# A mixer's output projection as seven Strassen products, with weight sums made in DRAM

## Chip, cores and metric

The kernel runs on one core of a Trainium2 chip. The time is the device time of one execution in microseconds (us), taken as the median of several runs; lower is better. Five engines run their own instruction streams: TensorE (PE in the rows, PEld for its weight loads), VectorE (DVE), ScalarE (ACT), GpSimd (POOL) and SyncE (SP), which here only issues DMA transfers.

## The reference, cut to what matters

One decoder layer on a sequence of 512 tokens with a width of 2048, all in float32: attention and a state-space branch are gated and merged, then comes an output projection with a norm and a residual, then a SwiGLU feed-forward network (FFN).

```python
merged = sigmoid(gate_a) * attn_branch + sigmoid(gate_s) * ssm_branch     # (512, 2048)
x = x + rms_norm(merged @ w_out, norm_mix_post)                           # w_out (2048, 2048)
h = rms_norm(x, norm_ffn_pre)
f = (silu(h @ w_ffn_gate) * (h @ w_ffn_up)) @ w_ffn_down                  # w_ffn_down (5632, 2048)
return x + rms_norm(f, norm_ffn_post)
```

## The kernel before

**Products in three passes.** Each float32 operand is split into a high part (ScalarE copies it into a reduced format) and a low part (VectorE subtracts the high part from the original). A product is high x high + high x low + low x high, three matmuls of 128x512. Weights arrive by SP's DMA queue in a ring of four tiles of 512 KB (`raw`); `split_hi` on ScalarE and `split_lo` on VectorE make `w_hi` and `w_lo`, two deep. The semaphores `landed`, `hi_ready`, `lo_ready` and `piece_done` tie them together: a load waits until the piece four before it is split, a split until the piece two before it is multiplied.

**The stages around the change**, in the order in which every engine runs them:

- *The query, key and value stage.* After each load SP also issues a copy of 512 KB from `w_ffn_down` to `v_d`, DRAM to DRAM (`v_begin`).
- *The gated-unit (GLU) stage*, 32 pieces in 8 turns of four, 693 us to 867 us. Each piece has a load and a `v_begin`. At the end of each turn from the second on GpSimd stores `sig_g` to `gl_d` (line 2834). `gate_sums` on VectorE prepares the mixer's units.
- *The mixer's units*, 14 of them, 867 us to 1140 us: Strassen products of gate weights, 7 products each. SP loads 2 MB for a unit (`load_unit`, line 695) while the unit before is multiplied; VectorE forms block sums of them (lines 2172 to 2182). After each second unit VectorE merges two rows of tiles into `au_c` (`merge_ssm`), GpSimd stores them to `m_d` and reloads `au_c` and `gl_c`.
- *The output projection*, 1140 us to 1314 us. `merged` comes back whole from `m_d` into `mrg` and is split into `a_hi` and `a_lo` in six runs (`MRG_RUNS`). Then come 32 pieces of 24 matmuls, in four column blocks of 512 over all four chunks of 128 tokens (`piece_t`). Beside a block's successor ScalarE squares it for the norm and VectorE multiplies it by the gain. The last four pieces run chunk by chunk (`last_mix_pieces`), so that chunk c is complete while chunk c+1 is multiplied.
- *Weight sums for the down projection.* During the output projection GpSimd issues six turns of `v_turn`. A turn is up to four transfers that add 512 KB from DRAM onto a `v_d` block (`accum_op`); each turn waits for the landing of the one before. The other turns run beside the FFN's units, spread over a turn by waits on `product`.
- *The middle norm.* For each chunk: `mix_gain`, mean, root, `mix_residual` (which makes `x2`), a square of `x2`, root and `x2_scale`. Then TensorE transposes the scaled chunks by pairs (`pe_mid_turn`), ScalarE and VectorE make high and low parts of the result, and the first four FFN pieces are multiplied in halves (`pe_mid_piece`), chunks 0 and 1 first.
- *The FFN's units*, then the *down projection*, which is already seven Strassen products (Z1 to Z7) of 22 steps each: a step (`piece_d`) has 12 matmuls on a block of 256 K-rows, a load of 512 KB and one of 128 KB; VectorE combines finished products in SBUF beside later steps (`combine`).

TensorE, ScalarE, VectorE, GpSimd and SP each run a fixed order written out by hand, so an instruction that waits holds all behind it on its engine.

## Time and profile before

| | |
|---|---|
| median of 3 runs | 2623.95 us (2623.66 to 2624.27) |
| the profiled execution | 2623.74 us, its span 2622.0 us |
| TensorE busy | 2598.7 us (99%) |
| VectorE, ScalarE, GpSimd busy | 1735.6, 1055.9, 590.4 us |
| DMA | 504.20 MB, mean 192 GB/s |

Busy time is a share of the span. TensorE's clock is granted at full speed nearly throughout. Matmuls overlap, so the time of one is longer than the spacing between two. The DMA share is the mean busy share of the core's 16 DMA engines; packet time of a queue is given as a share of the same 16 engines.

### The profile page before, as it was taken

The page shows a single profiled execution, that of the slowest core. Times are in us where ns is not written, and L with a number is a line of the kernel's source. Part 1 is how long each engine was busy: PE and PEld are TensorE (multiplying, and loading weights), DVE is VectorE, ACT ScalarE, POOL GpSimd, SP SyncE. Part 2 cuts the span into 40 slices and gives each one's busy share as a digit, 9 for nine tenths or more (in the row PEclk, how much of TensorE's full clock was granted, in tenths as well). Part 3 has the DMA queues.
Part 4 walks back from the last instruction along what each step waited for, and adds up shares of the span by engine and source line. Part 5 has one row for each costly group of instructions (what it writes and reads, how often), then busy time and mean ns, then how long its engine had stood idle before and what let it go on. Part 6 is the DMA issues. An engine that isn't in the chain of part 4 may idle for free.

```text
span 2622.0 us, 38782 instructions
## 1 busy us (share of the span) xinstructions
PE 2598.7 (99%) x14213; PEld 2222.4 (85%) x14213; DVE 1735.6 (66%) x2121; ACT 1055.9 (40%) x1427; POOL 590.4 (23%) x828
## 2 busy tenths in 40 slices
PE   8999999999999999999999999999999999999998
PEld 7888888888888888888888888888888888888887
DVE  5233232243344899962477999999999997666677
ACT  5222231232422444442354444444444444555555
POOL 3979127771000000001101212212212211000000
PEclk9999999999999999999999999999999999999999
DMA  6477676527666444378734586676677655788777
GB/s 186 137 229 229 168 188 217 194 70 206 217 218 209 151 153 161 128 255 194 177 128 146 156 213 179 169 213 184 169 207 191 181 148 195 257 272 277 242 242 237
DMA packets 310580, 504.20 MB, mean 192 GB/s; under 512 B 29024, under 2 KB 238304, under 8 KB 308032
## 3 DMA queue, kind: packets, MB, share of 16 engines
q1 hardware_dynamic: 264456, 365.76, 42.7%
q0 software_dynamic: 28720, 118.48, 18.3%
q10 hardware_dynamic: 17288, 18.40, 2.3%
q8 instruction: 74, 1.21, 0.2%
q14 instruction: 42, 0.34, 0.0%
HBM read 448.60 MB, written 150.41 MB: 228 GB/s over the span
## 4 chain that ended last, share of the span: by engine, by line
PE 95%; DVE 3%; issue 1%; ACT 1%; ACTq 0%; DVEq 0%
PE ps L787 26%; PE ps L793 14%; PE ps L495 8%; PE ps L499 8%; PE ps L497 8%; PE ps L851 5%; PE ps L853 5%; PE ps L855 5%; PE ps L616 2%; PE ps L617 2%; PE ps L618 2%; PE ps L603 1%; PE ps L602 1%; PE ps L601 1%; PE ps L583 1%
## 5 line engine op out<-in xcount | busy, mean ns | idle before, releaser
L483 DVE TENSOR_TENSOR w_lo<-raw,w_hi 128x1024 fp32r<-128x1024 f32 x176 | 229.8, 1306 | 539.9 <-ACT w_hi L479 539.8
L479 ACT ACTIVATE w_hi<-raw 128x1024 fp32r<-128x1024 f32 x176 | 186.5, 1060 | 559.0 <-PE ps L499 346.5
L495 PE MATMUL ps<-a_both,w_hi 128*128 128x512 f32 x640 | 252.4, 394 | 0.1
L497 PE MATMUL ps<-a_both,w_hi 128*128 128x512 f32 x640 | 249.4, 390 | 0.0
L499 PE MATMUL ps<-a_both,w_lo 128*128 128x512 f32 x640 | 249.4, 390 | 0.0
L787 PE MATMUL ps<-a_both,w_hi 128*128 128x512 f32 x872 | 216.9, 391 | 0.0
L787 PEld LDWEIGHTS ps<-a_both,w_hi 128*128 128x128 f32 x872 | 160.3, 188 | 31.1
L787 PE MATMUL ps<-a_both,w_hi_b 128*128 128x512 f32 x640 | 159.2, 391 | 0.0
L717 ACT ACTIVATE w_hi<-raw 128x1024 fp32r<-128x1024 f32 x81 | 85.5, 1056 | 165.7 <-DVE raw L2182 76.3
L495 PEld LDWEIGHTS ps<-a_both,w_hi 128*128 128x128 f32 x640 | 120.2, 188 | 27.6 <-issue 1.8
L499 PEld LDWEIGHTS ps<-a_both,w_lo 128*128 128x128 f32 x640 | 120.2, 188 | 25.1
L497 PEld LDWEIGHTS ps<-a_both,w_hi 128*128 128x128 f32 x640 | 120.3, 188 | 23.9
L808 ACT ACTIVATE f_hi<-f_raw 128x256 fp32r<-128x256 f32 x151 | 63.1, 418 | 188.0 <-PE ps L855 187.9
L787 PEld LDWEIGHTS ps<-a_both,w_hi_b 128*128 128x128 f32 x640 | 117.7, 188 | 22.7
L2885 POOL TENSOR_TENSOR f_sums<-f_t 128x256 f32<-128x256 f32 x22 | 34.5, 1569 | 450.2 <-DVE f_t L2439 363.4
L787 PE MATMUL ps<-s_both,w_hi_b 128*128 128x512 f32 x480 | 119.4, 391 | 0.0
L787 PE MATMUL ps<-s_both,w_hi 128*128 128x512 f32 x480 | 119.4, 391 | 0.0
L851 PE MATMUL ps<-w_hi,f_hi 128*128 128x512 f32 x300 | 116.8, 389 | 1.5 <-DVE f_lo L812 1.5
L851 PE MATMUL ps<-w_hi_b,f_hi 128*128 128x512 f32 x304 | 118.3, 389 | 0.0
L853 PE MATMUL ps<-w_lo_b,f_hi 128*128 128x512 f32 x304 | 118.3, 389 | 0.0
L855 PE MATMUL ps<-w_hi_b,f_lo 128*128 128x512 f32 x304 | 118.3, 389 | 0.0
L853 PE MATMUL ps<-w_lo,f_hi 128*128 128x512 f32 x300 | 116.8, 389 | 0.0
(439 smaller groups left out, 6458.2 us busy)
## 6 DMA issues: line engine op xcount, KB each, us to landing
raw<-in_w_in SPq DMA_DIRECT2D x108, 512.0 KB, 4.5
v_d<-in_w_ffn_down SPq DMA_DIRECT2D x88, 512.0 KB, 5.2
raw<-in_w_ffn_gate SPq DMA_DIRECT2D x88, 512.0 KB, 10.8
raw<-v_d SPq DMA_DIRECT2D x88, 512.0 KB, 4.9
raw_b<-in_w_ffn_up SPq DMA_DIRECT2D x80, 512.0 KB, 5.4
raw<-in_w_ffn_down SPq DMA_DIRECT2D x66, 512.0 KB, 4.8
v_d<-in_w_ffn_down POOLq DMA_DIRECT2D x44, 512.0 KB, 8.8
v_d<-v_d POOLq DMA_DIRECT2D x44, 512.0 KB, 7.8
```

The costliest lines, as they stand in the source:

```text
L479: nc.scalar.activation(w_hi[:, m % 2, :], raw[:, m % 4, :], ACT.Copy).then_inc(hi_ready, 1)
L483: nc.vector.tensor_tensor(w_lo[:, m % 2, :], raw[:, m % 4, :], w_hi[:, m % 2, :].bitcast(F32), ALU.subtract).then_inc(lo_ready, 1)
L495: nc.tensor.matmul(o, wh[:, k, cols], x_hi[:, kt0 + k, :], start=first and k == 0, stop=False, skip_group_check=halves)
L497: nc.tensor.matmul(o, wh[:, k, cols], x_lo[:, kt0 + k, :], start=False, stop=False, skip_group_check=halves)
L499: mm = nc.tensor.matmul(o, wl[:, k, cols], x_hi[:, kt0 + k, :], start=False, stop=last and k == 3, skip_group_check=halves)
L717: nc.scalar.activation(by_kt(ph.hi[ph.slot(j, i)]), operand(ph, j, i), ACT.Copy).then_inc(unit_hi, 1)
L787: mm = nc.tensor.matmul(wide, wh[:, k, :], ph.x_both[p][k], start=starts, stop=False, skip_group_check=True)
L793: mm = nc.tensor.matmul(o, wl[:, k, :], ph.x_hi[p][:, k, :], start=opens and p < 4 and k == 0, stop=False, skip_group_check=True)
L808: nc.scalar.activation(dst, f_raw[:, n % 4, :], ACT.Copy).then_inc(f_hi_ready, 1)
L851: nc.tensor.matmul(o, f_hi[n % 2][:, toks], wh[:, d, :], start=opens, stop=False, skip_group_check=True)
L853: nc.tensor.matmul(o, f_hi[n % 2][:, toks], wl[:, d, :], start=False, stop=False, skip_group_check=True)
L855: mm = nc.tensor.matmul(o, f_lo[n % 2][:, toks], wh[:, d, :], start=False, stop=closes, skip_group_check=True)
```

## The change

The output projection is computed as seven Strassen products over halves of tokens, K-rows and columns. K is cut into 8 pairs of 128-row tiles (`WO_PAIRS`), so there are 7 x 8 = 56 steps of 12 matmuls, in the order O1, O6, O7, O5, O4, O3, O2. Four of the products need weight sums and four need sums of `merged`.

- Weight sums: SP begins them by copies of `w_out` to `vo_d` (the first 32 of `v_begin`), which moves 32 later copies for `v_d` to the mixer's units, six after each unit's loads. GpSimd adds onto `vo_d` in ten turns (`vo_turn`): seven in the GLU stage behind the stores to `gl_d`, three in the mixer's units between the reloads of `au_c` and `gl_c`, where four turns of `v_turn` follow. Two more `v_turn` come at the start of the FFN; none is left in the output projection.
- Sums of `merged`: GpSimd makes four per pair (`merged_sums`) and stores them to `ms_d`.
- The stage: each step loads 128 KB of `ms_d` or `m_d` and 512 KB of weights; ScalarE and VectorE split both. `mrg` is not reloaded. Products are combined in `o_t` by 32 operations on VectorE and ScalarE; the last three steps are kept and multiplied chunk by chunk.
- The middle norm: chunks 2 and 3 come first, chunks 0 and 1 second. The scaling by the inverse root moves from VectorE to ScalarE (`act_x2_scale`), gains and residuals are done in halves of 1024 columns.

The core of the diff:

```diff
+WO_PAIRS = KT // 2
+WO_STEPS = 7 * WO_PAIRS
+B_FF = B_WO + WO_STEPS
 def v_begin(sp, i):
+            v, j, l = ((0, 0, 0), (2, 0, 1), (1, 1, 1), (3, 1, 0))[i % 4]
+            if i < 4 * WO_PAIRS:
+                sp.dma_start(vo_d[v][i // 4], w_block(w_out, j, l, i // 4)).then_inc(vo_begun, 16)
+            else:
+                m = i // 4 - WO_PAIRS
+                sp.dma_start(v_d[v][m], w_block(w_fd, j, l, m)).then_inc(v_begun, 16)
...
+            for u in range(MIX_UNITS):
+                g, j = u // 4, u % 4
+                load_unit(sp, MIX, g, j, w_in, 512 * g + (GA_COL, GS_COL)[j % 2] + 256 * (j // 2 + 1))
+                for i in range(88 + 6 * u, min(88 + 6 * u + 6, 4 * (WO_PAIRS + PAIRS))):
+                    v_begin(sp, i)
...
+            for n in range(WO_STEPS):
+                load_out(sp, n)
...
+            def vo_turn(t):
+                if t:
+                    pool.wait_ge(v_added, 16 * v_adds(t, WO_PAIRS))
+                else:
+                    pool.wait_ge(vo_begun, 16 * 4 * WO_PAIRS)
+                if t < WO_PAIRS:
+                    v_add(vo_d[0], t, w_block(w_out, 0, 1, t))
+                    v_add(vo_d[2], t, w_block(w_out, 1, 1, t))
+                if 1 <= t <= WO_PAIRS:
+                    v_add(vo_d[1], t - 1, vo_d[0][t - 1])
+                if 2 <= t < WO_PAIRS + 2:
+                    v_add(vo_d[3], t - 2, vo_d[1][t - 2])
...
             for it in range(1, 8):
                 pool.wait_ge(gl_made, it + 1)
                 pool.dma_start(gl_d[:, 2 * it:2 * it + 2, :].rearrange("p a n -> p (a n)"), sig_g[:, :]
                                ).then_inc(gl_stored, 16)
+                vo_turn(it - 1)
...
                     pool.dma_start(m_d[:, 2 * it - 2:2 * it, :], au_c[:, :, :]).then_inc(m_stored, 16)
+                    store_merged_sums(it - 1)
                     pool.wait_ge(m_stored, 16 * it)
...
                 pool.dma_start(au_c[:, :, :], au_d[:, kts, :]).then_inc(au_in, 16)
+                if it <= 3:
+                    vo_turn(6 + it)
+                else:
+                    v_turn(it - 4)
                 pool.wait_ge(gl_stored, 16 * it)
                 pool.dma_start(gl_c[:, :, :], gl_d[:, kts, :]).then_inc(gl_in, 16)
...
+            for n in range(WO_STEPS - ENDS):
+                piece_o(pe, n)
+            out_end_pieces(pe)
...
+            out_end_hi(act, 0)
+            act_x2_square(act, 0)
+            out_end_hi(act, 1)
+            out_end_hi(act, 2)
+            act_mid_root(act, 2, 0)
+            act_x2_scale(act, 0)
+            for i in range(4):
+                act_mix_square(act, 8 + i, i // 2, 2 + i % 2, AFTER_O3)
+            act_x2_square(act, 1)
             for m in (B_FF, B_FF + 1):
                 kept_split_hi(act, m)
+            act_mid_root(act, 3, 1)
+            act_x2_scale(act, 1)
+            split_hi(act, B_FF + 2, 0)
+            split_hi(act, B_FF + 3, 0)
+            act_mix_square(act, 12, 0, 0, AFTER_O3 + 1)
+            act_mix_square(act, 13, 0, 1, AFTER_O3 + 2)
+            act_mid_root(act, 4, 2)
...
+            out_end_lo(dve, 0)
+            mix_root(1, 1)
+            mix_residual(1, 0, 4)
+            out_end_lo(dve, 1)
+            x2_mean(0)
+            out_end_lo(dve, 2)
+            mix_residual(1, 1, 4)
+            x2_invert(2, 0)
+            mix_gain(0, 1, 10)
+            mix_gain(1, 1, 12)
+            last_product(0, 0)
+            last_product(0, 1)
+            x2_mean(1)
             for m in (B_FF, B_FF + 1):
                 kept_split_lo(dve, m)
+            x2_invert(3, 1)
+            split_lo(dve, B_FF + 2, 0)
+            split_lo(dve, B_FF + 3, 0)
+            mix_gain(0, 0, 14)
+            mix_mean(2)
+            last_product(1, 0)
+            last_product(1, 1)
```

## Rows read from the trace of the kernel before

**Rows 1.** The page, chain that ended last: share of the span by engine.
```profile
PE 95%; DVE 3%; issue 1%; ACT 1%; ACTq 0%; DVEq 0%
```

**Rows 2.** Output projection's first matmul line; ns min/median/max, first and last start.
```profile
L616 PE MATMUL ps<-w_hi,a_both x224: 388/389/467, 1140.3 to 1292.0; 128*128 128x512 f32 x112
```

**Rows 3.** Windows: busy us of PE, PEld, DVE, ACT, POOL; clock, DMA share, GB/s.
```profile
742.00:850.00 108.00, 108.00 (x478) 89.49 (x477) 52.16 (x45) 33.35 (x33) 2.36 (x5) 1.00 0.65 213
850.00:871.00 21.00, 21.00 (x102) 17.69 (x101) 13.23 (x13) 6.71 (x7) 0.53 (x1) 1.00 0.39 127
871.00:910.00 39.00, 39.00 (x227) 34.48 (x226) 36.18 (x44) 18.43 (x25) 1.60 (x3) 1.00 0.55 188
910.00:1105.00 195.00, 195.00 (x1123) 172.38 (x1122) 187.99 (x225) 89.82 (x121) 8.02 (x15) 1.00 0.44 148
1314.00:1348.00 34.00, 31.55 (x255) 29.79 (x254) 23.75 (x48) 20.09 (x45) 0.58 (x1) 1.00 0.41 156
2290.00:2400.00 110.00, 110.00 (x487) 91.12 (x486) 73.46 (x93) 54.91 (x80) 1.62 (x3) 1.00 0.81 271
```

**Rows 4.** The adds' DMA queue, 1206 to 1250 (packets, MB, share); one load.
```profile
q0 software_dynamic: 1152, 4.19, 53.1%
...
L451 SPq DMA_DIRECT2D raw<-in_w_out x1: 373/373/373, 1208.4 to 1208.4; - x1
...
DMA to landing us min/median/max: 12.0/12.0/12.0
```

**Rows 5.** SP's DMA queue in the GLU stage, 785 to 829.
```profile
q1 hardware_dynamic: 5481, 8.50, 59.1%
```

**Rows 6.** SP's DMA queue in the mixer's units, 910 to 1105.
```profile
q1 hardware_dynamic: 21120, 20.97, 32.9%
```

**Rows 7.** Timeline of issues: start us, us, queue; SP's, then GpSimd's.
```profile
837.24 0.38 SPq L451 DMA_DIRECT2D raw<-in_w_glu_g  x1
...
853.69 5.81 SPq L695 DMA_DIRECT2D raw<-in_w_in  x2
...
867.69 2.85 SPq L695 DMA_DIRECT2D mix_raw_b<-in_w_in  x4
...
881.47 2.04 SPq L695 DMA_DIRECT2D raw<-in_w_in  x4
...
872.36 0.53 POOL L2834 DMA_DIRECT2D gl_d<-sig_g  x1 [21.39 <-DVE sig_g L2102]
```

**Rows 8.** Timeline: readers of loads, then TensorE around the stage's end.
```profile
856.65 1.06 ACT L479 ACTIVATE w_hi<-raw 128x1024 fp32r<-128x1024 f32 x1 [4.38 <-PE ps L499]
...
864.27 1.22 DVE L2175 TENSOR_TENSOR raw<-raw 128x1024 f32<-128x1024 f32 x1
...
884.83 1.22 DVE L2175 TENSOR_TENSOR mix_raw_b<-mix_raw_b 128x1024 f32<-128x1024 f32 x1
...
904.33 1.22 DVE L2175 TENSOR_TENSOR raw<-raw 128x1024 f32<-128x1024 f32 x1
...
1314.48 0.27 PE L1001 MATMUL ps<-ident,o_t 128*128 128x128 f32 x1
...
1318.24 0.39 PE L515 MATMUL ps<-a_both,r_hi 128*128 128x256 f32 x1 [0.34 <-DVE a_both L1868]
```

**Rows 9.** Timeline of the middle norm, ScalarE and VectorE.
```profile
1298.35 0.60 ACT L1365 ACTIVATE sq_t<-ps 128x512 f32<-128x512 f32 x1 [2.42 <-PE ps L568]
...
1305.60 1.90 ACT L1371 ACTIVATE o_t<-x 128x2048 f32<-128x2048 f32 x1
...
1299.07 0.69 DVE L2326 TENSOR_TENSOR o_t<-ps,gain_b 128x512 f32<-128x512 f32 x1 [1.51 <-ACT sq_t L1365]
...
1305.93 2.35 DVE L2336 SCALAR_TENSOR_TENSOR x<-o_t,stat,x 128x2048 f32<-128x2048 f32 x1
...
1316.52 1.66 DVE L1868 SCALAR_TENSOR_TENSOR a_both<-ps,gain_t,a_both 128x256 fp32r<-128x256 f32 x4
```

**Rows 10.** The page's group of the FFN's pair sums on GpSimd.
```profile
L2885 POOL TENSOR_TENSOR f_sums<-f_t 128x256 f32<-128x256 f32 x22 | 34.5, 1569 | 450.2 <-DVE f_t L2439 363.4
```

More of the change, by code:

```diff
@@ L398, in build @@
         gl_in = sem("gl_in")
-        mrg_in = [sem(f"mrg_in{h}") for h in range(2)]
+        vo_begun = sem("vo_begun")
+        x2_inverse = sem("x2_inverse")
         gs_made = sem("gs_made")
@@ L857, in piece_d @@
[L857 to L870 removed]
+            step(pe, n, B_DN, WO_STEPS, f_hi, f_lo, q, m == 0 and q != Z2, m == PAIRS - 1)
@@ L878, in end_pieces @@
                 for i in range(ENDS):
-                    part(1, d, i)
+                    mm = end_part(1, d, i, e_hi, e_lo, ef_hi, ef_lo)
+                mm.then_inc(down, 1)
         def w_tiles(w, row_tiles, rows0, cols0, n):
@@ new lines, in _, with mix_gain, mix_mean @@
+            out_lo(dve, 2)
+            out_lo(dve, 3)
+            def mix_gain(c, half, squares):
+                dve.wait_ge(mix_sq, squares)
+                dve.wait_ge(gb_in[0], 16)
+                cols = slice(1024 * half, 1024 * half + 1024)
+                tt(o_t[:, c, cols], o_t[:, c, cols], gain_b[:, cols], ALU.mult).then_inc(mix_gained, 1)
+            def mix_mean(i):
+                c = OUT_ORDER[i]
+                dve.wait_ge(mix_sq, (4, 8, 14, 16)[i])
+                link(nc.vector.tensor_reduce(stat[:, 0, c:c + 1], sq_part[:, :, c], AX, ALU.add))
+                ts(stat[:, 1, c:c + 1], stat[:, 0, c:c + 1], 1.0 / D, EPS, ALU.mult, ALU.add).then_inc(rstd_in, 1)
@@ new lines, in mix_root, with mix_residual @@
+            def mix_root(n, i):
+                c = OUT_ORDER[i]
+                dve.wait_ge(rstd_sqrt, CLS + n + 1)
+                link(nc.vector.reciprocal(stat[:, 2, c:c + 1], stat[:, 1, c:c + 1]))
+            def mix_residual(i, half, gains):
+                c, cols = OUT_ORDER[i], slice(1024 * half, 1024 * half + 1024)
+                dve.wait_ge(mix_gained, gains)
+                dve.wait_ge(x_again, 16 * CLS)
+                added = stt(x2[:, c, cols], o_t[:, c, cols], stat[:, 2, c:c + 1], x2[:, c, cols], ALU.mult, ALU.add)
+                if half:
+                    added.then_inc(x2_ready, 1)
@@ new lines, in x2_mean, with x2_invert, last_product @@
+            def x2_mean(i):
+                c = OUT_ORDER[i]
+                dve.wait_ge(sq_done, CLS + i + 1)
+                ts(stat[:, 1, c:c + 1], stat[:, 0, c:c + 1], 1.0 / D, EPS, ALU.mult, ALU.add).then_inc(rstd_in, 1)
+            def x2_invert(n, i):
+                c = OUT_ORDER[i]
+                dve.wait_ge(rstd_sqrt, CLS + n + 1)
+                nc.vector.reciprocal(stat[:, 2, c:c + 1], stat[:, 1, c:c + 1]).then_inc(x2_inverse, 1)
+            def last_product(c, d):
+                if c == 0 and d == 0:
+                    dve.wait_ge(mixed, 1)
+                else:
+                    dve.wait_ge(piece_done, B_FF - ENDS + 2 * c + d)
+                combine(AFTER_O3 + 2 * c + d, o_part(c, d), o_part(c, d), down_bank(O2, c, d), ALU.add)
@@ new lines, in _ @@
+            for n in range(4, WO_STEPS - ENDS):
+                out_lo(dve, n)
+                dve_beside_out(n)
+            out_end_lo(dve, 0)
[11 more added lines that the diff above has]
+            x2_mean(1)
@@ L2553, in finish_part @@
                     ALU.add).then_inc(out_ready, 1)
-            def combine(done, out, a, b, op):
-                dve.wait_ge(combined, done)
-                tt(out, a, b, op).then_inc(combined, 1)
             def dve_beside(n):
@@ L2828, in _, with store_merged_sums @@
+            def store_merged_sums(m):
+                pool.wait_ge(gl_stored, 16 * 7)
+                pool.wait_ge(ms_stored, 16 + 32 * (m - 1))
+                merged_sums(m, au_c, *(ms_three[:, i, :] for i in range(3)), ms_last[:, :])
+                pool.dma_start(ms_d[m, :, 0:3, :], ms_three[:, :, :]).then_inc(ms_stored, 16)
+                pool.dma_start(ms_d[m, :, 3, :], ms_last[:, :]).then_inc(ms_stored, 16)
             pool.wait_ge(au_copied, 8)
```

590 lines of the change are left out of this document (309 added, 281 removed).

## The prediction

> **What bounds the kernel now.** The page comes first. TensorE is busy for 99% of the span and makes 95% of the chain that ended last [rows 1]; so the end moves only with TensorE's work or with a wait that reaches it. The profiled execution took 2623.74 us for a span of 2622.0, 1.7 us outside it, and lies 0.2 us under the median of 2623.95; I add to and subtract from that median. A difference of 0.2% (5.2 us) is about what this kernel's measurement can tell from none.
>
> The second view gives the stage that is replaced. Its 768 matmuls of 128x512 run from 1140.2 to the first transpose of the middle norm at 1314.5 with TensorE busy throughout [rows 2, 8]: 174.2/768 = 0.2268 us each. Nothing but TensorE limits that stage.
>
> The third view is the DMA share of each stage, since the change multiplies DRAM traffic. It is 0.65 in the gated-unit (GLU) stage from 742 to 850, 0.39 to 871, then 0.55 and 0.44 in the mixer's units, while TensorE has no gap in any of them [rows 3]. The last rows show how the middle norm hides: its ScalarE and VectorE steps run per chunk under matmuls, so that the stretch from 1314 to 1348 has only 2.45 us of idle TensorE [rows 3].
>
> **The change, part by part.**
>
> *Matmuls.* 56 steps of 12 matmuls are 672 in place of 768: 96 x 0.2268 = **-21.8 us**. This is certain if nothing waits.
>
> *Loads of the new stage.* A step needs 640 KB in 12 x 0.2268 = 2.72 us. The down projection already has this very shape, and ran with no TensorE gap at a share of 0.81 with a spill beside it [rows 3]. I cost these loads at nothing; without that cover each late load would show as a gap before its step.
>
> *Start of the stage.* VectorE has the last merge (two 1.2 us operations after a sigmoid, the width of the row of 884.8 [rows 8]) before the split of step 2; by its queue that split ends some 1 us after step 2 could start. I take **+1**, bounds 0 and, if both of the last splits come one operation later, 3.
>
> *DRAM adds.* What one costs is read in the stage where six turns of them stand today. The two turns between 1206 and 1250 have 8 adds, whose queue took 53.1% of 44 us: 2.9 us of all 16 engines each, 11.7 us for a turn of four [rows 4]. In the GLU stage SP's queue spends 59.1% of 44 us on 8 pairs of load and copy, 3.25 us a pair [rows 5]; in the mixer's units its 40 loads take 32.9% of 195 us, 1.6 each [rows 6]. So a DRAM copy costs 1.65.
>
> The change puts turns of 2, 3, 4, 4, 4 and 4 adds behind the stores of the GLU stage, some 21.8 us apart; the seventh and last store is issued at 872.4 [rows 7], so the first at about 742, and behind the seventh turn stands an eighth at once; and SP issues six copies (9.9 us) after the loads of each of the first five units. Of each 21.8 us a full turn wants: 0.65 x 21.8 = 14.2 used today, + 11.7 = 25.9. That is more than there is. Backlog: about 1 after the turn of 763.5, 5 at 807, 9 at 829, 13 at 850.4. The last GLU load is issued at 837.2 and first read at 856.7 [rows 7, 8], so with 4 us to land and 3 before TensorE misses it the slack is some 18 us, and these pieces just pass. Then:
> - unit 0's last load is issued at 859 [rows 7] and VectorE reads it from 864.3 [rows 8]; product 1 starts late once it lands after 867. Behind 13 of backlog, one turn (11.7), a store (1.3) and 3.2 of loads, from 850.4 on, it lands near 880: **13 us late**.
> - unit 1's loads (issued 867.7 [rows 7], the second half first read at 884.8 [rows 8]) stand behind six copies: 9.9 + 6.4, and the turn of 872.4 with its neighbours, 14. From 880 that is 910, against 884.8 + 13: **12 more**.
> - unit 2's loads (issued 881.5 [rows 7]) stand behind six copies, with the eighth turn: 910 + 16.3 + 12.8 = 939; the second half is read at 904.3 [rows 8], now + 25 = 929: **10 more**.
> - unit 3's, 19.5 us on, are due near 958 and land near 957; unit 4's, with two adds, are late by some **2**. After that the backlog melts: the share of 0.44 leaves 22 us free in 39 [rows 3].
>
> The sum is 37. It has every load land last of what was issued before it. One load issued 2.3 us after a burst of four adds took 12.0 us to land [rows 4], and the burst with the loads in it some 4 x 2.9 + 3 x 1.5 = 16, so a load is nearly last but not quite. I take **+32**; bounds: 0 (the slack absorbs all; below nothing is excluded, since TensorE has no idle there to give back) and 45 (GLU pieces late too). The Trainium skill (DMA: Bandwidth & Descriptors, section on queues, rings and completion order) says that each DMA engine takes turns between its queue rows, a whole packet at a time. By that rule the adds would lengthen a load by the packets interleaved and not by the whole burst, and my 37 would be some 26; the landing of 12.0 us is nearer to the burst.
>
> *Sums of the merged rows on GpSimd.* Four operations at the 1.57 us of the FFN's pair sums [rows 10] and two stores before the next reload of au_c: 7 us more, where the reader of that reload comes some 19 us after the merge before it. They run beside VectorE, which is busy 187.99 of 195 us there [rows 3]. Cost 0, upper bound 5 (the 7 us of VectorE's idle time gone, less a little).
>
> *The adds that leave the output stage.* TensorE had no gap there [rows 3], so this returns 0. Two turns now fall at the FFN's first pair sums; the share there leaves room: 0, up to 3.
>
> *The tail and the middle norm.* This is the part to follow in the queues. Durations [rows 9]: ScalarE 2.0 for a square of a chunk with its sum read, as a scale of one about 1.9, 0.75 for a square of a quarter; VectorE 2.35/2 = 1.2 for a residual of half a chunk, 0.7 for a combine, 1.66/4 = 0.4 for the residue of a turned tile; and 1.06 on ScalarE for a weight half [rows 8]. Times from E, where matmul 672 would end unhindered. VectorE has beside steps 50 to 52 a combine, two half-chunk residuals and a gain over 2.72 us a step, 1.7 us of slack: the splits for the last three steps are done near -7.3, -4.3 and -2.5, where TensorE wants them at -8.2, -6.8 and -5.4. The last matmul ends at **+3**.
>
> Chunk 3 (second in the new order) is scaled only after: residual of chunk 3 (-1.3), scale of chunk 2 (+0.9), four quarter squares (+3.9), square of chunk 3 (+5.9), two weight splits (+8.0), VectorE's residues for them and the reciprocal (+9.4), scale (+11.4). The first transposes wait for it: idle from +3 to +11.5. Then ScalarE has two weight splits and two squares (+14.9), VectorE gain, mean and the last two combines (+17.7), which free the banks of transposes 4 and 5; the turned tiles are ready and piece 0 starts at **+19.5**. Today it starts at 1318.2, 3.8 after the end of the matmuls [rows 8]. Between, chunks 0 and 1 still need residual, square, scale: waits of 2.4, 2.6 and 0.8 us at pieces 1, 3 and the second transposes, less some 1.3 that today's pieces wait. In all (19.5 - 3.8) + 4.5 = **+20**, the tail's 3 within it; bounds 8 (if the scale of chunk 3 is ready at once, and only the last two chunks' chain remains) and 26.
>
> Sum: 2624 - 21.8 + 1 + 32 + 20 = **2655 us**.
>
> **Rivals.**
> - *DMA absorbs it.* What speaks for it: loads have a unit of lead, and a share is no hard limit. Against: every share above is time of all 16 engines, and 0.65 + 0.54 is over one. Then 2624 - 21.8 + 1 + 20 = **2623**, no change; chance 0.14.
> - *The norm hides and only DMA costs*: the tail and norm cost 5; 2624 - 21.8 + 1 + 32 + 5 = **2640**; chance 0.12.
> - *Faster.* The saving of matmuls stands because neither reaches TensorE: the loads land before their readers, and chunks 2 and 3 are normed before the last steps end. It decides on whether chunk 3's scale comes before +5 and unit 1's loads before 885. 2624 - 21.8 + 1 + 5 = **2608**; chance 0.17. For it: chunks 2 and 3 are complete 22 us before the end; against it: the four squares and two splits placed ahead of that scale.
> - *My case*, both: **2655**, own range 2632 to 2680; chance 0.57.
>
> **The numbers.** The range goes from 2612 (leaving out most of the faster case) to 2680 (the upper bounds of either large cost). Faster by over 0.2% is the faster case and a quarter of the first rival: 0.21; within 0.2%: 0.07, about half of the first rival; slower: 0.72.
>
> **What would show it.** Matmuls of the output stage: 672 at 0.227, some 153 us. TensorE's gaps between 850 and 990: 32 us if the adds and copies count, with ScalarE or VectorE named as waiting for a load; none if they are absorbed. The DMA share from 785 to 950 should be near 0.95. Between the last output matmul and piece 0: some 16 us; transposes waiting for ScalarE's scale of o_t. The prediction is wrong if the share from 785 to 910 stays under 0.9, or if the first middle transpose follows the last matmul at once.

## The result, and the profile after

The changed kernel takes 2666.59 us (median of 4 runs, 2664.46 to 2667.43) against 2623.8 us before it: 1.016 times as long, 95% interval 1.0148 to 1.0173. The forecast was 2655 us with a range of 2612 to 2680 and a chance of 0.72 for slower. The sign and the range held; how the sum came about did not hold everywhere. The profiled execution has a span of 2664.5 us, 42.5 more than before's 2622.0.

The first view answers to [rows 3]: the stages in windows (same columns).

```profile
742.00:850.00 108.00, 108.00 (x478) 89.41 (x478) 52.15 (x46) 33.35 (x33) 16.94 (x22) 1.00 1.00 283
850.00:871.00 21.00, 18.16 (x80) 14.79 (x79) 8.09 (x8) 3.18 (x3) 3.96 (x5) 0.99 1.06 305
871.00:910.00 39.00, 31.91 (x160) 27.41 (x159) 27.03 (x32) 15.52 (x19) 8.51 (x11) 0.83 1.04 297
910.00:949.00 39.00, 31.16 (x162) 26.96 (x161) 28.08 (x32) 12.81 (x16) 6.48 (x8) 0.87 1.01 337
949.00:1105.00 156.00, 151.07 (x858) 132.52 (x857) 151.49 (x174) 68.32 (x92) 30.52 (x38) 0.99 0.68 210
1179.00:1341.00 162.00, 155.47 (x671) 126.51 (x672) 118.19 (x156) 90.17 (x144) 8.49 (x12) 0.99 0.79 264
1341.00:1391.00 50.00, 35.05 (x260) 31.93 (x259) 32.17 (x62) 32.92 (x63) 0.54 (x1) 0.86 0.34 127
```

The DMA share is 1.00 from 742 to 850 in the GLU stage, where it was 0.65, and above 1.0 from there to 949. From 850 to 949 TensorE is idle for 17.8 us (2.84 + 7.09 + 7.84), where it had no gap, and its granted clock is down to 0.83 and 0.87 of full speed from 871 on. Who is waited for is in the next view, the timeline of TensorE (what ended the idle time stands in brackets), and in VectorE's waits from 860 to 950 (us in total, times, longest):

```profile
870.17 3.24 PE L830 MATMUL ps<-a_both,w_hi 128*128 128x512 f32 x8 [2.84 <-ACT w_hi L760]
...
896.03 3.75 PE L830 MATMUL ps<-a_both,mix_hi_b 128*128 128x512 f32 x8 [6.83 <-DVE sg L2336]
...
926.07 2.04 PE L836 MATMUL ps<-a_both,w_lo 128*128 128x256 f32 x8 [7.84 <-DVE sg L2336]
```

```profile
DVE mix_t_sum L2259 <- issue: 18.8, 2, 9.9
DVE mix_t_sum L2259 <- DMA raw<-in_w_in: 8.8, 1, 8.8
```

There are three gaps, one for each of the first units, as the prediction had them, and the load of a unit's weights is what VectorE lacks. The profile names the load at one of its three waits only; at the other two it names nothing ("issue"). But these operations start at 892.9 and 923.0, and the second load of the unit, issued at 869.3 and 896.3, took 23.6 and 26.6 us to land, which is 892.9 and 922.9 (before, these loads took 3.5 to 7.6 us). Behind each gap the matmuls run at half clock for a while. That shows in the rows too: eight matmuls of 128x512 take 3.24 and 3.75 us, where the same row at full clock reads 2.0.

The pace of the units is read from the stores of the merged pairs: count, first and last start. Before, then after:

```profile
L2840 POOL DMA_DIRECT2D m_d<-au_c x6: 536/536/538, 915.6 to 1110.8; - x6
```

```profile
L3027 POOL DMA_DIRECT2D m_d<-au_c x6: 543/564/564, 940.1 to 1149.0; - x6
```

The first store is 24.6 us late: 17.8 of idle time and some 7 of slower matmuls. That is the DMA term. But from the first store to the sixth it is 208.9 us in place of 195.2, so that another 13.7 us come in after the backlog is gone (share 0.68). The prediction has nothing there. The timeline of VectorE and of GpSimd at one of these stores says what it is:

```profile
1063.26 2.71 DVE L765 TENSOR_TENSOR w_lo<-raw,w_hi 128x1024 fp32r<-128x1024 f32 x1
1065.89 1.76 DVE L2269 TENSOR_TENSOR raw<-raw 128x1024 f32<-128x1024 f32 x1
1067.57 1.76 DVE L2259 TENSOR_TENSOR mix_t_sum<-mix_raw_b 128x1024 f32<-128x1024 f32 x1
1069.25 1.21 DVE L765 TENSOR_TENSOR mix_lo_b<-raw,mix_hi_b 128x1024 fp32r<-128x1024 f32 x1
...
1063.43 0.76 POOL L2996 TENSOR_TENSOR ms_three<-au_c 128x256 f32<-128x256 f32 x1
1064.12 0.75 POOL L2997 TENSOR_TENSOR ms_three<-au_c 128x256 f32<-128x256 f32 x1
1064.95 1.61 POOL L2999 TENSOR_TENSOR ms_three<-au_c,ms_three 128x256 f32<-128x256 f32 x1
1066.64 1.61 POOL L3001 TENSOR_TENSOR ms_last<-ms_three,au_c 128x256 f32<-128x256 f32 x1
```

VectorE's operation of this shape takes 1.22 us, here 2.71, 1.76 and 1.76 while GpSimd subtracts: 2.6 us lost for each set of four subtractions.

The new output stage runs from 1179.0 to the first transpose at 1341.35: 162.3 us against 174.2. The 672 matmuls alone are 152.4, so 9.9 are waits: 6.5 us idle in the window above, 1.4 in seven matmuls at half clock (0.43 us apart in place of 0.23) behind the longest of these gaps, and 2.0 in wider spacing here and there. In the middle the timelines of TensorE and ScalarE read:

```profile
1341.12 0.39 PE L927 MATMUL ps<-we_hi,wef_lo 128*128 128x512 f32 x1
...
1349.41 1.76 PE L1077 MATMUL ps<-ident,o_t 128*128 128x128 f32 x7 [7.79 <-ACT o_t L1450]
...
1354.86 2.33 PE L1077 MATMUL ps<-ident,o_t 128*128 128x128 f32 x8 [3.70 <-DVE o_t L2360]
1357.22 0.58 PE L524 MATMUL ps<-a_both,w_hi_b 128*128 128x256 f32 x1
```

```profile
1336.94 2.01 ACT L1450 ACTIVATE o_t<-x,stat 128x2048 f32<-128x2048 f32 x1 [2.54 <-DVE stat L2419]
...
1341.92 1.89 ACT L1437 ACTIVATE o_t<-x 128x2048 f32<-128x2048 f32 x1
...
1347.35 2.00 ACT L1450 ACTIVATE o_t<-x,stat 128x2048 f32<-128x2048 f32 x1 [1.46 <-DVE stat L2419]
```

Between the two scales (L1450) lie the four quarter squares, chunk 3's square and two weight splits, in that order; the transposes wait for the second scale. Piece 0 starts 16.1 us after the last output matmul. From the first transpose to the first matmul behind the middle pieces it is 49.6 us (1341.4 to 1391.0) against 34.1 (1314.5 to 1348.5). The transposes by themselves, first and last start, are a shorter measure of the same stretch, 28.2 us before and 43.7 after:

```profile
L1001 PE MATMUL ps<-ident,o_t x64: 270/273/328, 1314.5 to 1342.7; 128*128 128x128 f32 x64
```

```profile
L1077 PE MATMUL ps<-ident,o_t x64: 270/273/477, 1341.4 to 1385.1; 128*128 128x128 f32 x64
```

So the 42.5 us are: DMA 24.6, units after that 14.1 (to the output stage's start), output stage -11.9 (-21.8 + 9.9), middle +15.6, rest 0.1.

### The profile page after: what moved, and what is told of

It reads as the page before. It is cut to its first block, busy times and chain, and to the rows that moved or that the text cites. A ratio compares the mean times of both kernels' runs of the same rounds, so it can differ in the third digit from the quotient of the medians.

```text
span 2664.5 us, 39011 instructions
## 1 busy us (share of the span) xinstructions
PE 2594.7 (97%) x14117; PEld 2212.0 (83%) x14117; DVE 1803.4 (68%) x2224; ACT 1100.8 (41%) x1509; POOL 665.8 (25%) x909
## 4 chain that ended last, share of the span: by engine, by line
PE 47%; DVE 2%; ACT 1%; issue 0%; DVEq 0%; ACTq 0%
PE ps L830 19%; PE ps L836 10%; PE ps L891 5%; PE ps L893 5%; PE ps L895 5%; PE ps L504 1%; PE ps L508 1%; PE ps L506 1%; ACT o_t L1437 0%; DVE x_b L2683 0%; PE ps L524 0%; PE ps L528 0%; PE ps L526 0%; ACT o_t L1450 0%; PE ps L1077 0%
## 5 line engine op out<-in xcount | busy, mean ns | idle before, releaser
L492 DVE TENSOR_TENSOR w_lo<-raw,w_hi 128x1024 fp32r<-128x1024 f32 x146 | 192.6, 1320 | 449.7 <-ACT w_hi L488 449.6
L488 ACT ACTIVATE w_hi<-raw 128x1024 fp32r<-128x1024 f32 x146 | 154.5, 1059 | 451.4 <-PE ps L508 346.2
L760 ACT ACTIVATE w_hi<-raw 128x1024 fp32r<-128x1024 f32 x81 | 85.6, 1056 | 174.3 <-DVE raw L2269 81.8
L508 PEld LDWEIGHTS ps<-a_both,w_lo 128*128 128x128 f32 x640 | 120.1, 188 | 25.4
L836 PEld LDWEIGHTS ps<-a_both,w_lo 128*128 128x128 f32 x872 | 114.2, 193 | 12.5 <-DVE w_lo L765 8.0
L836 PE MATMUL ps<-a_both,w_lo 128*128 128x256 f32 x872 | 116.8, 285 | 7.8 <-DVE sg L2336 7.8
```

What stands on the lines that cost most here:

```text
L488: nc.scalar.activation(w_hi[:, m % 2, :], raw[:, m % 4, :], ACT.Copy).then_inc(hi_ready, 1)
L492: nc.vector.tensor_tensor(w_lo[:, m % 2, :], raw[:, m % 4, :], w_hi[:, m % 2, :].bitcast(F32), ALU.subtract).then_inc(lo_ready, 1)
L508: mm = nc.tensor.matmul(o, wl[:, k, cols], x_hi[:, kt0 + k, :], start=False, stop=last and k == 3, skip_group_check=halves)
L760: nc.scalar.activation(by_kt(ph.hi[ph.slot(j, i)]), operand(ph, j, i), ACT.Copy).then_inc(unit_hi, 1)
L836: mm = nc.tensor.matmul(o, wl[:, k, :], ph.x_hi[p][:, k, :], start=opens and p < 4 and k == 0, stop=False, skip_group_check=True)
```

## The experiments

Measured beside these runs, before took 2623.8 to 2624.1 us. "First store" and "last store" are those of the two rows above; 915.6 and 1110.8 before, 940.1 and 1149.0 after.

### Is it the DRAM traffic? Traffic alone, and a part of it moved

**e1_traffic**: the kernel before, with the copies and adds where the change puts them.

```diff
             for it in range(1, 8):
                 pool.dma_start(gl_d[...], sig_g[:, :]).then_inc(gl_stored, 16)
+                vo_turn(it - 1)
...
+                for i in range(88 + 6 * u, min(88 + 6 * u + 6, 4 * (WO_PAIRS + PAIRS))):
+                    v_begin(sp, i)
```

> The kernel before, with the change's DRAM traffic and nothing else of it: the copies of the output weights ahead of those of the down weights (so six copies stand behind the loads of each of the first units), the turns of adds behind the GLU stage's stores and beside the mixer's units, no turns in the output stage. The sums of the output weights are made and not used; the output projection and the norm are those of before. Theory (the 16 DMA engines are asked for more than they have from 785 on): the first gated unit's end comes 24 to 28 us late with DMA shares of about 1.0 from 763 to 950, and the time is 2648 to 2654. First rival (the lateness up to 940 us comes from the added work on the engines, not from the transfers): within 3 us of 2624. Second rival (transfers are late, but the turns that left the output stage give something back there): below 2645.

Measured: 2658.37 us, ratio 1.0136 (1.0119 to 1.0153). Its windows from 742 on:

```profile
742.00:850.00 108.00, 108.00 (x479) 89.41 (x478) 51.97 (x45) 33.47 (x33) 17.10 (x22) 1.00 1.00 282
...
871.00:910.00 39.00, 26.73 (x130) 22.90 (x131) 24.13 (x28) 12.77 (x16) 8.47 (x11) 0.78 1.03 291
...
949.00:1105.00 156.00, 156.00 (x899) 137.86 (x898) 150.22 (x181) 72.16 (x96) 17.97 (x26) 1.00 0.68 208
```

The first store is at 941.0, 25.4 late, with the same shares and the same fall of the clock; the transfers alone do it. After 949 there is no gap: the later drift is not theirs. The time is 4 us over what was expected, because this kernel, which still reloads the merged rows before its output stage, waits 5.4 us for VectorE's split there, at 1172, with a turn of four adds and the reload issued from 1142 to 1156. That the adds are its cause is only argued.

**e3_copies_later**: the changed kernel with the 32 copies behind the mixer's unit loads moved to the middle stage's loads.

```diff
-                for i in range(88 + 6 * u, min(88 + 6 * u + 6, ...)):
-                    v_begin(sp, i)
             for k in range(16):
                 load(sp, B_FF + k, ...)
+                for i in (88 + 2 * k, 89 + 2 * k):
+                    v_begin(sp, i)
```

> The changed kernel, with the 32 copies that stand behind the unit loads of the mixer moved to the loads of the middle stage (two behind each), where the DMA share is 0.36 to 0.43. Theory of the prediction (the copies make units 1 and 2 late, 22 of 37 us by its count, and the adds unit 0): the first pair of units comes 12 to 18 us earlier than in the changed kernel, and the time is 2646 to 2654. Rival (the adds alone take what there is, and the copies only ride along): not below 2661.

Measured: 2660.55 us, the median of three runs (2653.75, 2660.55, 2663.97), ratio 1.0126 (1.0106 to 1.0147); a fourth run of 12720.78 us, for which the record has no cause, is left out. The first store came at 925.7, 14.4 earlier, as the theory said, and the lead was still 12.0 us at the last middle transpose. In the profiled run, the slowest of the three, only 2.3 us of it are left at the end. Windows from 1400 on:

```profile
1400.00:1440.00 40.00, 40.00 (x178) 33.14 (x177) 21.31 (x14) 11.21 (x10) 10.92 (x9) 1.00 1.01 305
1460.00:1480.00 20.00, 12.98 (x64) 10.87 (x63) 10.13 (x13) 5.63 (x8) 0.00 (x0) 0.83 0.97 261
```

Copies and turns 4 and 5 of the adds now meet there at a share of 1.01, a load of the FFN lands 7.0 us late for TensorE, and the clock falls: the same mechanism at another place. The copies are worth 14.4 of the 24.6 us and the adds 10.2, but copies moved as a block take most of their cost along. The time decides nothing: it lies between the theory's range and the rival's, with one run inside the theory's. The landmarks show that the cause was right and that the gain was mostly lost again.

### The drift after 949: GpSimd's arithmetic

**e2_sums**: the kernel before, with `merged_sums` and its stores: one set at 722.8 in the GLU stage, six beside the pairs of units. **e6_stores_only**: the same stores without the subtractions. **e10_sums_twice**: the subtractions of e2_sums made twice.

```diff
                     pool.dma_start(m_d[:, 2 * it - 2:2 * it, :], au_c[:, :, :]).then_inc(m_stored, 16)
+                    store_merged_sums(it - 1)
```

In e6_stores_only `store_merged_sums` is this, where `t` is `au_c` seen as four rows of 256:

```diff
-                merged_sums(m, au_c, *(ms_three[:, i, :] for i in range(3)), ms_last[:, :])
-                pool.dma_start(ms_d[m, :, 0:3, :], ms_three[:, :, :]).then_inc(ms_stored, 16)
+                pool.dma_start(ms_d[m, :, 0:3, :], t[:, 0:3, :]).then_inc(ms_stored, 16)
```

and in e10_sums_twice the four subtractions stand in a loop:

```diff
+                for r in range(2):
                     tt(s1, f21, f22, ALU.subtract).then_inc(ms_made, 1)
                     tt(s3, f11, f21, ALU.subtract).then_inc(ms_made, 1)
```

> The kernel before, with GpSimd's four subtractions of the merged rows and their two stores to DRAM beside each pair of units (seven sets), and nothing else of the change; the sums are not used. Theory (VectorE's operations take longer while GpSimd's run, and VectorE has only 7 us of idle time in 195): VectorE operations next to a set show 1.7 to 2.7 us in place of 1.22, each pair of units grows by 1 to 2 us once the idle time is gone, and the time is 2629 to 2635. Rival (what grew by 13.5 us between 940 and 1149 in the changed kernel came from late transfers): within 1.5 us of 2624.

> The kernel before with the same stores to DRAM as in e2_sums and without GpSimd's subtractions (the stores read the merged rows themselves; nothing reads what they write). It tells the arithmetic from the transfers and from the later reload of au_c. Theory (GpSimd's arithmetic slows VectorE's): within 2 us of 2623.9. Rival (the stores, or the reload that comes later behind them, made e2_sums slower): 2630 or more.

> e2_sums with each set of four subtractions made twice (same operands, same results, not used), the stores once. Theory (each set takes some 2.5 us from VectorE, whose idle time in the units is 1.4 us a pair; the cost goes with the number of subtractions beyond it): e2_sums gave 10.9 us over before, twice the sets give 26 to 32 us over it, 2650 to 2656. Rival (the cost is one of order, the reload of au_c being late behind the sums, so that it grows by GpSimd's own 6 us a pair only where that reaches a reader): below 2643.

| | us | last store | ratio (95%) |
|---|---|---|---|
| e6_stores_only | 2623.75 | 1110.5 | 0.9999 (0.9990 to 1.0009) |
| e2_sums | 2634.79 | 1119.1 | 1.0041 (1.0027 to 1.0055) |
| e10_sums_twice | 2643.37 | 1126.0 | 1.0073 (1.0056 to 1.0090) |

The transfers cost nothing and the arithmetic 10.9 us. Windows of 40 us, first of e2_sums, then of e6_stores_only:

```profile
990.00:1030.00 40.00, 38.24 (x218) 33.38 (x218) 39.03 (x45) 16.82 (x23) 7.38 (x9) 1.00 0.47 152
```

```profile
990.00:1030.00 40.00, 40.00 (x231) 35.27 (x230) 38.61 (x48) 18.65 (x25) 2.70 (x5) 1.00 0.47 157
```

VectorE is busy longer and does less (45 operations in place of 48). Neither e2_sums nor e10_sums_twice has a wait of VectorE for the reload of `au_c` among its rows from 910 to 1140, so a late reload isn't the cause there.

For twice the sets I had expected 26 to 32 us. It gave 19.6, at the edge of what the rival allowed. The rows say why. In e2_sums the six sets beside the units stretch VectorE's operations by 2.5 us each (the fifth by 1.6), 14.2 in all, of which 10.9 reached the end. The repeats in e10_sums_twice add only 1.1 us each, 21.2 in all, of which 19.6 reached the end. So VectorE's idle time absorbs 3 us at most, and a repeat is cheaper than a first set, because part of it falls beside operations that aren't stretched. In e10_sums_twice, VectorE and then GpSimd:

```profile
1091.45 0.41 DVE L2260 TENSOR_TENSOR mix_q<-mix_p,ps 128x256 f32<-128x256 f32 x1
1091.90 0.42 DVE L2262 TENSOR_TENSOR mix_q<-mix_q,ps 128x256 f32<-128x256 f32 x1
1092.35 1.25 DVE L2266 TENSOR_TENSOR sg<-sg,mix_q 128x512 f32<-128x512 f32 x1
...
1091.61 0.74 POOL L2841 TENSOR_TENSOR ms_three<-au_c 128x256 f32<-128x256 f32 x1
1092.31 0.74 POOL L2842 TENSOR_TENSOR ms_three<-au_c 128x256 f32<-128x256 f32 x1
```

The two operations with an input from PSUM (`ps`) keep their 0.41 us beside a running subtraction. The next one, which reads two SBUF tiles, takes 1.25 us in place of 0.69.

### The middle norm

**e4_norm_order**: the changed kernel, order of the two engines' steps alone.

```diff
-            for i in range(4):
-                act_mix_square(act, 8 + i, i // 2, 2 + i % 2, AFTER_O3)
             act_x2_square(act, 1)
-            for m in (B_FF, B_FF + 1):
-                kept_split_hi(act, m)
+            act_mix_square(act, 8, 0, 2, AFTER_O3)
             act_mid_root(act, 3, 1)
+            act_mix_square(act, 9, 0, 3, AFTER_O3)
             act_x2_scale(act, 1)
+            ...
+            act_mid_turn(act, 0, range(4))
+            for m in (B_FF, B_FF + 1):
+                kept_split_hi(act, m)
```

> The changed kernel, with the middle norm's steps in another order on ScalarE and VectorE: chunk 3's square and scale ahead of the quarter squares and of the weight splits, the last combines ahead of the gains, chunk 0 before chunk 1, the first turned tiles ahead of the splits. Theory (the first transposes wait for work queued ahead of chunk 3's scale, piece 0 for what is queued ahead of the turned tiles): the idle before the first transposes falls from 7.8 to about 3.5, piece 0 starts 9 to 10 us after the last output matmul in place of 16, and the time is 2658 to 2662. Rival (the chain from the last combine through the banks sets piece 0, whatever the order; or chunks 0 and 1 are then late by what is won): within 2 us of 2666.6.

Measured: 2665.85 us (2661.51 to 2667.73), not told from 2666.6, as the rival had it in its second form (chunks 0 and 1 are then late by what is won). TensorE's timeline:

```profile
1344.13 2.15 PE L1077 MATMUL ps<-ident,o_t 128*128 128x128 f32 x11 [2.78 <-ACT o_t L1450]
...
1349.86 0.55 PE L524 MATMUL ps<-a_both,w_hi_b 128*128 128x256 f32 x1 [1.28 <-DVE w_lo_b L548]
...
1363.21 1.12 PE L1077 MATMUL ps<-ident,o_t 128*128 128x128 f32 x4 [3.83 <-DVE a_both L1955]
```

Piece 0 starts 7.4 us earlier, so the order of the queue was its cause. Then a turned tile that stands behind chunk 0's square on ScalarE is late by 3.8 us, and the pieces run at half clock twice in place of once. Most of the gain is given back in the same stage.

### The same transfers, spread

**e5_spread**: the changed kernel, the same copies and adds at another pace: the adds for `w_out` in smaller bursts, the 32 copies and all adds for the down weights moved out of the mixer's units to the FFN.

```diff
-                vo_turn(it - 1)
+                vo_adds(*((0, 2), (2, 4), (4, 6), (6, 7), (7, 8), (8, 9), (9, 10))[it - 1])
...
-                if it <= 3:
-                    vo_turn(6 + it)
-                else:
-                    v_turn(it - 4)
+                vo_adds(*((10, 14), (14, 18), (18, 22), (22, 26), (26, 29), (29, 31), (31, 32))[it - 1])
...
+                    if g <= 8:
+                        v_begin(sp, 88 + 4 * (g - 1) + j)
...
+                v_turn(m + 1, PROD0 + 14 * m + 85 if 2 <= m < PAIRS - 2 else None)
```

**e7_spread_norm**: e5_spread with the norm's order of e4_norm_order, tiles 8 to 11 turned earlier.

```diff
             act_mix_square(act, 15, 1, 1, AFTER_O2)
+            act_mid_turn(act, 0, range(8, 12))
             act_x2_square(act, 2)
-            act_mid_turn(act, 0, range(8, 12))
```

**e8_no_sums**: e7_spread_norm with the stores of e6_stores_only; it leaves out the sums of the merged rows, so the output isn't the reference's. **e9_adds_first**: e7_spread_norm, with the adds issued ahead of the sums and the turns of the FFN one pair earlier.

```diff
                     pool.dma_start(m_d[:, 2 * it - 2:2 * it, :], au_c[:, :, :]).then_inc(m_stored, 16)
+                    vo_adds(*adds)
                     store_merged_sums(it - 1)
...
-                v_turn(m + 1, PROD0 + 14 * m + 85 if 2 <= m < PAIRS - 2 else None)
+                v_turn(m + 2, PROD0 + 14 * m + 85 if 2 <= m < PAIRS - 2 else None)
```

> The changed kernel with the same DRAM copies and adds, spread out: behind the stores of the GLU stage two, two, two and then one add each, beside the mixer's units four, four, four, four, three, two and one in place of four each and six copies behind each unit's loads; the 32 late copies stand four to a group behind the loads of the FFN's units, and the adds for the down weights run one turn for each of the FFN's pairs. Theory (the DMA engines were asked for more than they have in one stretch; the amount as such can be hidden): DMA share under 0.95 in every window from 742 to 1150, no TensorE gap over 2 us and no half clock from 850 to 990, first store of a merged pair at 915 to 920, time 2636 to 2644. Rival (what is moved comes back as late loads where it now stands, as it did with the 32 copies moved as one block): above 2652.

> e5_spread with the middle norm's steps reordered once more: as in e4_norm_order, and tiles 8 to 11 turned on ScalarE before chunk 0's square, the later weight split of VectorE behind them. Theory (in e4_norm_order 5 of the 7.5 us won at piece 0 were given back in one wait of 3.8 us for turned tile 9 and its half clock): no gap over 1 us between piece 0 and the first transposes of chunks 0 and 1, time 3 to 6 us under e5_spread. Rival (ScalarE and VectorE are full there, so that any order gives the same end): within 1.5 us of e5_spread.

> e7_spread_norm without GpSimd's sums of the merged rows: the stores take the merged rows as they are, so that the four products that want the sums compute something else. All transfers and matmuls stay. Theory (the sums cost VectorE's time in the units, 10.9 us in the kernel before): 8 to 12 us under e7_spread_norm, the stores of merged pairs 39.0 us apart again in place of 41 to 44. Rival (with the transfers spread, VectorE's idle time hides them): within 2 us of e7_spread_norm.

> e7_spread_norm with two changes of order on GpSimd's queue: beside the mixer's units the adds are issued right behind the store of the merged pair and ahead of the sums and the reload, and in the middle and the FFN the turns for the down weights run one pair earlier, so that none of four adds is left for the start of the down projection. Theory (in e5_spread and e7_spread_norm the sums put the adds 6 us later, where they met the next unit's load: VectorE waited 3.2 us for it in each of three pairs; and the last turns made a load of the down projection late by 2.6 us): pairs 40.5 to 42 us apart in place of 43.8, the output stage starts at 1148 to 1153 in place of 1160.6, the rest 3 to 4 us shorter, time 2632 to 2639. Rival (the sums cost 20 us once the transfers are spread, wherever the adds stand): above 2643.

| | us | first, last store | output stage from | ratio (95%) |
|---|---|---|---|---|
| e5_spread | 2651.19 | 915.4, 1129.8 | 1160.5 | 1.0101 (1.0084 to 1.0118) |
| e7_spread_norm | 2647.63 | 915.8, 1129.9 | 1160.6 | 1.0096 (1.0079 to 1.0113) |
| e8_no_sums | 2627.19 | 915.6, 1110.8 | 1140.1 | 1.0011 (1.0001 to 1.0020) |
| e9_adds_first | 2637.60 | 915.4, 1124.2 | 1154.0 | 1.0052 (1.0035 to 1.0068) |

With the transfers spread the first store is where it was before the change: all 24.6 us of the DMA term are gone from there. They aren't all gone from the time: behind the last middle transpose e5_spread takes 1283.6 us, where before takes 1279.3, with a wait of TensorE of 2.5 us at 2239.8, in the down projection, that before doesn't have. Windows of e5_spread:

```profile
742.00:850.00 108.00, 108.00 (x478) 89.42 (x477) 52.13 (x46) 33.34 (x33) 9.37 (x13) 1.00 0.84 252
...
871.00:910.00 39.00, 39.00 (x226) 34.46 (x225) 36.16 (x44) 18.46 (x25) 5.93 (x8) 1.00 0.92 255
```

The time is 7 us over what was expected all the same, since each of the first three pairs of units now took 44 us where GpSimd's sums account for 2 over 39. e8_no_sums shows that the sums set off all of it: without them every store is within 0.05 us of before's, and the kernel is 20.4 us faster. That is twice what the sums cost alone, because they also put the four adds 6 us later, where they met the next unit's load. In e5_spread's waits of VectorE from 970 to 1000:

```profile
DVE mix_t_sum L2259 <- DMA raw<-in_w_in: 3.2, 1, 3.2
```

e8_no_sums also says what the rest of the change is worth when neither DMA nor sums cost anything in the units. Its output stage takes 158.1 us (16.1 saved), its middle 42.0 us from first to last transpose (13.8 lost), and 4.5 are lost behind that: the norm alone eats most of the saving.

e9_adds_first takes part of that back: a pair in 41.8 us, the output stage 6.6 earlier, 10.0 us in all, and behind the last middle transpose it takes 1279.4 us, as before. The adds ahead of the reload have a price of their own: VectorE now waits for `au_c`, 7.3 us in three times. e7_spread_norm gained 3.6 us in the median, with ranges that overlap (2644.1 to 2652.3, and 2648.0 to 2652.6), and not where I expected it: from the first to the last transpose it took 42.8 us, e5_spread 43.7, as chunk 1's scale was late by 5.0 us instead. What the two profiles differ by lies in the output stage ahead, 156.8 us in place of 160.7, which the edit doesn't touch. There e5_spread has a gap of 2.05 us at 1205.0, behind a load of `vo_d` for which ScalarE waited 4.2 us (1.9 in e7_spread_norm, without a gap), and seven matmuls at half clock behind it. Why that load landed earlier in one of two executions is open.

### A version that pays

**e11_dma_sums**: e9_adds_first, where the sums of pairs 1 to 6 are made without GpSimd's arithmetic, and where four quarter squares fill ScalarE's waits before the last output matmul.

```diff
+                        nc.scalar.activation(ms_three[:, 0:2, :], au_c[:, :, quad[1]], ACT.Copy, scale=-1.0)...
+                        nc.scalar.activation(ms_three[:, 2, :], au_c[:, 1, quad[0]], ACT.Copy, scale=-1.0)...
+                        nc.scalar.activation(ms_last[:, :], au_c[:, 1, quad[1]], ACT.Copy)...
...
+                    ms_add(m, slice(1, 4), ms_three[:, 0, :], 3)
+                    ms_add(m, slice(0, 1), ms_three[:, 1, :], 1)
...
             out_end_hi(act, 2)
+            act_mix_square(act, 8, 0, 2, AFTER_O3)
+            act_mix_square(act, 9, 0, 3, AFTER_O3)
+            act_mix_square(act, 10, 1, 2, AFTER_O3)
             act_mid_root(act, 2, 0)
```

**e12_two_bursts**: e11_dma_sums, with two of each four adds behind the pair's last sum.

```diff
-                    vo_adds(*adds)
+                    vo_adds(adds[0], min(adds[0] + 2, adds[1]))
...
                     ms_add(m, slice(3, 4), ms_three[:, 2, :], 1)
+                    if adds[1] > adds[0] + 2:
+                        vo_adds(adds[0] + 2, adds[1])
```

> e9_adds_first with two changes. First, the sums of the merged rows of pairs 1 to 6 are no longer made by GpSimd: ScalarE, which is busy 18 of 39 us there, writes negated copies of three quarter rows (and one plain copy), and the sums arise in DRAM by accumulating transfers, seven quarter rows a pair; GpSimd still makes the first and the last set. Second, in the middle norm the four quarter squares whose inputs are complete early go into ScalarE's waits before the last matmul, and VectorE scales chunk 1 into its residual earlier. Theory (VectorE loses its time to GpSimd's arithmetic, not to the transfers): pairs 39.0 to 39.6 us apart in place of 40 to 43, output stage from 1141 to 1144; the middle (first to last transpose) 36 to 40 us in place of 42.8; time 2616 to 2624, so the change as a whole would just begin to pay. Rival (the added transfers, some 5 us of all engines a pair, or the later reload of au_c make loads late again): above 2628.

> e11_dma_sums with the adds for the output weights split: two behind the store of a merged pair, the other two behind the last of the pair's sums, some 30 us later. In e11_dma_sums VectorE's operations kept their 1.22 us, but it waited 3.9 to 4.3 us for the reload of au_c, which was issued behind four adds, and TensorE for it. Theory (the reload lands in time behind two adds): no such wait over 1 us, pairs 39.0 to 40.2 us apart, the output stage starts at 1141 to 1146 in place of 1152.4, time 2619 to 2624. Rival (the accumulating transfers of the sums themselves keep the reload late): within 3 us of 2630.

e11_dma_sums measured 2630.10 us, ratio 1.0024 (1.0015 to 1.0033), as the rival had it. The operations of VectorE keep 1.22 us, and the middle takes 36.2 us; but in its waits from 880 to 1145 the first row, which e9_adds_first had with 7.3 us, has grown:

```profile
DVE au_c L2309 <- DMA au_c<-au_d: 11.6, 4, 4.3
```

The reload of the pair stood behind four adds. e12_two_bursts measured 2619.46 us (2614.89 to 2623.94), ratio 0.998 (0.997 to 0.9989): 4.6 us less than before it. Its windows and its transposes:

```profile
871.00:910.00 39.00, 39.00 (x226) 34.47 (x225) 36.18 (x45) 18.46 (x25) 5.96 (x8) 1.00 0.90 249
...
949.00:1105.00 156.00, 156.00 (x898) 137.83 (x897) 150.01 (x181) 76.05 (x108) 40.41 (x49) 1.00 0.92 236
```

```profile
L1077 PE MATMUL ps<-ident,o_t x64: 270/273/474, 1296.9 to 1333.6; 128*128 128x128 f32 x64
```

TensorE has no gap in the units at a share of 0.90 to 0.92, with more transfers there than the changed kernel has from 949 on. The output stage starts at 1139.9, as before the change, and takes 157.0 us in place of 174.2; the middle, first to last transpose, 36.7 in place of 28.2. Some 5.7 us are lost behind it, where one unit's load of the FFN is 3.6 us late for TensorE; that wasn't pursued.

## Why the prediction was right, and which steps of it were wrong

- *Matmuls, -21.8*: right. 672 matmuls at 0.2268.
- *Start of the stage, +1, and tail, +3*: 4 in all, measured 9.9 for the stage's waits. TensorE was idle 5.1 us at three steps for the row split of VectorE (`wo_f_lo`), most of it early in the stage, and 1.4 at the tail; half clock and wider spacing make the rest. Mis-sized by some 6. The longest wait, 3.1 us at step 2 (1187.8), is the mechanism of the +1: the splits stood behind the last merge, which ended at 1185.7. The row split also took 0.95 us in place of 0.42, beside GpSimd's last set of sums. The next wait, 1.7 us at 1226.8, is one of a load: ScalarE had waited 3.9 us for a block of `vo_d`. I had costed the loads of the stage at nothing.
- *DRAM adds and copies, +32*: the mechanism was right (e1_traffic, e5_spread), the size 24.6. Three units were late, with 2.8, 6.8 and 7.8 us of idle time in place of 13, 12 and 10; the rest of the 24.6 came from the clock, which the sum didn't have. That every load lands last of all that was issued before it was too strict: the last loads of units 0, 1 and 2 landed at 871.2, 899.3 and 925.6, where I had 880, 910 and 939. The rule of the Trainium skill (DMA: Bandwidth & Descriptors, queues, rings and completion order) gave an estimate of 26, for which I showed no working, and was nearer than the row I leaned on, though that figure too leaves the clock out. Of the split within: copies 14.4 (e3_copies_later), adds 10.2; I had 22 and 13.
- *Sums on GpSimd, 0, bound 5*: the step that failed. From the first store to the output stage 14.1 us came in with them in the changed kernel, and they cost 10.9 by themselves (e2_sums), both outside the bound. I took "they run beside VectorE" from two separate queues and asked only whether the reload of au_c comes late. The row for GpSimd's pair sums at 1.57 us [rows 10] held a hint that can be read only now: the same line's shortest in the kernel before is 0.73 us and its median 1.65, so the 1.57 is mostly the time of an operation that waits for VectorE. The Trainium skill (SBUF — State Buffer, "SBUF: two separate sides") states it: VectorE and GpSimd share a pair of SBUF ports under an exclusive lock, which a VectorE operation with two SBUF inputs and a GpSimd operation that reads SBUF both want. The trace agrees: the stretched rows are those with two SBUF inputs, 2.71 in place of 1.22 beside two GpSimd operations of 0.75, and those with an input from PSUM keep their 0.41 (e10_sums_twice).
- *Adds leaving the output stage, 0*: right as far as shown; nothing was given back.
- *Tail and middle norm, +20*, tail's 3 included: the norm's 17 came as 15.6. Piece 0 was forecast 16 us after the last matmul and started at 16.1; the reason, work queued ahead of chunk 3's scale, is what e4_norm_order undid (7.8 us of idle time to 2.8).

The sum was 31.2 us over before and came as 42.5. DMA was 7.4 too high, sums 14.1 and the output stage's waits 5.9 too low, norm 1.4 too high. That the total missed the forecast by only 11 us owes something to luck: an oversized DMA term hid half of a term put at nothing. Of the signs named beforehand, the share (near 0.95) was passed, the 16 us held, and the gaps of 32 us from 850 to 990 were 17.8 of idle and 7 of slow matmuls.

## What to carry to other kernels

Transfers that were queued as blocks cost 24.6 us; metered, and in part moved to stages with room, they made no unit's load late once GpSimd's sums no longer delayed them (e8_no_sums), and some 4 us came back in the down projection until the turns ahead of it were moved as well (e9_adds_first). Moving a block as a block mostly moves the late load; follow each gain to the end of the trace before believing it. An idle engine isn't free to use: before giving GpSimd arithmetic on SBUF, look whether VectorE has idle time in that stage and which of its operations would run beside it, and count what each set stretches (here 2.5 us, or 1.1 for a repeat).

## What the runs showed of the hardware that was not expected

TensorE's granted clock halved in or behind gaps of 3 to 8 us. In the changed kernel the clock column is 1.00 in the window before the first gap and 0.83 and 0.87 in the windows with the larger ones, and eight 128x512 matmuls behind a gap take 3.24 and 3.75 us: 1.2 GHz in place of 2.4. In windows of 1 us the clock reads 0.50 for 3.4, 10.2 and 10.2 us. The first of these stretches lies behind its gap of 2.8 us; the other two begin 2.0 us and 3.7 us into gaps of 6.8 and 7.8, so that matmuls ran slowly for 5.4 and 6.1 us of them. Before has no such gap and a mean clock of 0.999, after 0.991. So a late load costs its wait and some us more: 17.8 us of gaps made the first store 24.6 late. e12_two_bursts has no gap in the units and shows 1.00 there.

GpSimd's subtraction of 128x256 took 0.75 us or 1.61 us in one set of four, with VectorE's operation beside it at 2.71 or 1.76 us in place of 1.22; VectorE's operations with an input from PSUM kept their time beside it. ScalarE's work beside VectorE stretched nothing: with its copies added (e11_dma_sums) VectorE's operations keep 1.22 us.
